# Latent attention of a diffusion layer on one core: values in three split passes, normalisation moved to the output, scores in four PSUM banks

## The reference

```python
def one_block(qi):                      # 128 queries, all heads
    s = jnp.einsum('bqkgd,bskd->bkgqs', qi, k).astype(jnp.float32) * scale
    p = jax.nn.softmax(s, axis=-1).astype(v.dtype)
    return jnp.einsum('bkgqs,bskd->bqkgd', p, v)
...
merged = jax.nn.sigmoid(ga) * (attn @ lp['w_branch_a']) + jax.nn.sigmoid(gb) * (pool @ lp['w_branch_b'])
x = x + gt1 * (merged @ lp['w_out'])
```

## Time and profile before

| | |
|---|---|
| median of 3 runs | 1750.43 us (1743.49 to 1750.63) |
| profiled execution | 1748.0 us, its span 1746.2 us |
| TensorE busy | 1593.9 us (91%) |
| VectorE, ScalarE, GpSimd busy | 899.4, 593.2, 287.0 us |
| latent attention | from about 614 to 1019 us of the span |

### The profile page before, as it was taken

The page is one execution under the profiler, slowest core; times in us unless marked ns, Lnnn a source line. Parts: engine busy times, 40 slices in busy tenths (PEclk is TensorE's granted clock), DMA queues, the critical chain, the costliest instruction groups (busy, mean ns, idle before and its releaser), DMA issues. The chain is left out here.

```text
span 1746.2 us, 21787 instructions
## 1 busy us (share of the span) xinstructions
PE 1593.9 (91%) x8173; PEld 1260.8 (72%) x8173; DVE 899.4 (52%) x1350; ACT 593.2 (34%) x776; POOL 287.0 (16%) x214
## 2 busy tenths in 40 slices
PE   4899999999998979999999999999997699999950
PEld 3688888788887756666666678887886588888840
DVE  6570000025654366667666653333455666676629
ACT  5212111233222354444444442111222255555513
POOL 1011111112324210001000000000000145444420
PEclk9999999999999989999999999999998699999985
DMA  9143333221001030003000024326003388998935
GB/s 363 70 154 130 143 149 141 91 90 44 24 24 61 1 115 1 0 0 145 1 0 0 1 86 148 138 73 230 36 37 133 128 276 269 285 300 262 283 72 230
DMA packets 48983, 206.60 MB, mean 118 GB/s; under 512 B 4913, under 2 KB 13985, under 8 KB 39713
## 3 DMA queue, kind: packets, MB, share of 16 engines
q1 hardware_dynamic: 39712, 172.30, 26.2%
q0 software_dynamic: 9216, 33.56, 8.6%
HBM read 158.60 MB, written 47.24 MB: 118 GB/s over the span
## 5 line engine op out<-in xcount | busy, mean ns | idle before, releaser
L343 PE MATMUL psum<-h_hi,w_hi 128*128 128x512 f32 (+1 forms) x768 | 201.6, 371 | 9.9 <-DVE h_lo L755 5.5
L343 PE MATMUL psum<-h_lo,w_hi 128*128 128x512 f32 (+1 forms) x768 | 193.4, 360 | 0.0
L343 PE MATMUL psum<-h_hi,w_lo 128*128 128x512 f32 (+1 forms) x768 | 192.8, 359 | 0.0
L1268 PE MATMUL psum<-probT,vals 128*128 128x512 f32 x384 | 190.9, 593 | 0.0
L1416 ACT ACTIVATE prob<-psum,nmax 128x1536 f32<-128x1536 f32 x64 | 98.7, 1542 | 199.7 <-DVE nmax L1544 199.5
L343 PEld LDWEIGHTS psum<-h_hi,w_hi 128*128 128x128 f32 x768 | 129.2, 191 | 39.0 <-issue 18.5
L1284 PEld LDWEIGHTS psum<-ident,prob 128*128 128x128 f32 x768 | 93.7, 142 | 77.7 <-issue 71.6
L343 PEld LDWEIGHTS psum<-h_lo,w_hi 128*128 128x128 f32 x768 | 128.8, 190 | 23.1
L343 PEld LDWEIGHTS psum<-h_hi,w_lo 128*128 128x128 f32 x768 | 128.4, 189 | 23.0
L1541 DVE TENSOR_REDUCE rmax<-psum 128x1 f32<-128x512 f32 x192 | 129.3, 689 | 24.6 <-PE psum L1260 24.4
L653 POOL TENSOR_TENSOR w_lo<-w_raw,w_hi 128x1024 fp32r<-128x1024 f32 x32 | 77.1, 2410 | 340.0 <-ACT w_hi L517 340.0
(11 more groups left out here) (330 smaller groups left out, 2885.7 us busy)
## 6 DMA issues: line engine op xcount, KB each, us to landing
gu_raw<-in_w_gu SPq DMA_DIRECT2D x16, 2048.0 KB, 9.2
ada<-in_w_ada SPq DMA_DIRECT2D x20, 1024.0 KB, 4.8
w_raw<-in_w_in SPq DMA_DIRECT2D x16, 1024.0 KB, 4.8
dn_raw<-in_w_dn SPq DMA_DIRECT2D x16, 1024.0 KB, 6.8
gates<-gst SPq DMA_DIRECT2D x14, 640.0 KB, 3.0
y_sum<-stage SPq DMA_DIRECT2D x12, 512.0 KB, 5.6
xt<-in_x SPq DMA_DIRECT2D x10, 512.0 KB, 8.0
merged<-gates SPq DMA_DIRECT2D x8, 640.0 KB, 3.9
```

Of the source, the lines that this page charges most:

```text
L343: mm = pe.matmul(psum[:, par_sets[j] + g:par_sets[j] + g + w], a[j][:, k, :], b[:, k, g:g + w], start=(k == 0 and a is w_hi and b is h_hi) ...
L1268: mm = pe.matmul(psum[:, PV + 512 * x.par:PV + 512 * x.par + 512], vals[:, x.key0 // P + c, x.kv * HD:(x.kv + 1) * HD], probT[b][g % 2][:] ...
```

## The change

What it does:

- Values: the value tile is split into `v_hi` and `v_lo`, the turned probabilities into `pT_hi` (a copy on ScalarE, all three banks) and `pT_lo` (a subtraction on VectorE). Each chunk's product is three float32r passes. The last pass raises `a_pv_unit` itself. All outputs go to one bank.
- Normalisation: the probabilities stay as the exponential leaves them. One reciprocal of all four sums of a unit on VectorE; TensorE transposes each, read as a 128x128 tile by broadcasting, into bank 3 (SPREAD), ScalarE copies that to `inv_row`, and VectorE multiplies the output with it into `qT`.
- Scores: banks 0 to 3. An even head uses 0, 1, 2; an odd one 3, 1, 2 in that order of keys, so the first third of a head is written while the exponential before still reads.
- The maximum of the first two banks is taken before the third; scale and last maximum are one instruction.
- Values of the first group are split before unit 0 is done, those of the second in the step of unit 8 (`second`).
- Buffers move: the late gates, the raw pool inputs. SP's queue loads fewer of them early, and pool inputs 2 and 3 after unit 14 is turned; three waits are added ahead of merge loads.

The diff, cut to its core:

```diff
-        SC, TP, PV = 0, 1536, 3072
+        TP, PV, SPREAD = 2048, 3584, 1536
...
         def scores_at(x, g):
-            return SC + 1536 * (isinstance(x.u, int) and x.u == 0 and g % 2)
+            return g % 2 * (2048 if first_unit(x) else 512)
+        def keys_at(g, b):
+            return 512 * ((b + 2) % 3 if g % 2 else b)
...
@@ SP
-                for q in range(4):
+                for q in range(2):
                     sp.dma_start(wb_raw[q][:], io["w_merge_b"][q]).then_inc(b_in[q], 16)
...
+                sp.dma_start(pool_raw[0][:], io["poolT"][0]).then_inc(loaded[0], 16)
+                for b in range(3):
+                    sp.wait_ge(s[f"a_turned{b}"], GRP * 15)
+                for k in range(2, 4):
+                    sp.dma_start(pool_raw[k][:], io["poolT"][k]).then_inc(loaded[k], 16)
...
@@ TensorE
+                    if not first_unit(x):
+                        if g == 1:
+                            pe.wait_ge(s["a_row"], x.u)
+                        pe.wait_ge(s["a_exped"], 4 * x.u + g - 1)
...
                     for b in range(3):
+                        if b == 1 and not first_unit(x):
+                            pe.wait_ge(s["a_exped"], 4 * x.u + g)
...
-                    pe.wait_ge(s[f"a_t_out{b}"], m + 1)
-                    mm = pe.matmul(psum[:, PV + 512 * x.par:PV + 512 * x.par + 512], vals[...], probT[b][g % 2][:], ...)
-                    mm.then_inc(s[f"a_pv{b}"], 1)
-                    if c == x.keys // P - 1:
-                        pe.wait_ge(s[f"a_pv{b}"], m + 1)
-                        pe.sem_inc(s["a_pv_unit"], 1)
+                    if c == 0:
+                        pe.wait_ge(s["a_v_lo"], GRP * (x.kv + 1))
+                        pe.wait_ge(s["a_pv_out"], x.u + 1)
+                    pe.wait_ge(s[f"a_t_hi{b}"], m + 1)
+                    pe.matmul(o, v_hi[v], pT_hi[b][g % 2][:], start=(c == 0), stop=False)
+                    pe.matmul(o, v_lo[v], pT_hi[b][g % 2][:], start=False, stop=False)
+                    pe.wait_ge(s[f"a_t_lo{b}"], m + 1)
+                    mm = pe.matmul(o, v_hi[v], pT_lo[b][g % 2][:], start=False, stop=last)
+                    if last:
+                        mm.then_inc(s["a_pv_unit"], 1)
...
-                            pe.wait_ge(s[f"a_t_out{b}"], uses(x, g))
+                        pe.wait_ge(s[f"a_t_lo{b}"], uses(x, g))
...
                 def tail(x):
+                    pe.wait_ge(s["a_inv"], x.u + 1)
...
+                    for h in range(GRP):
+                        o = SPREAD + h * P
+                        mm = pe.transpose(psum[:, o:o + P], einv[:, x.par, h:h + 1].broadcast_to([P, P]), ident[:])
+                    mm.then_inc(s["a_spread"], 1)
                     for c in range(x.keys // P)[-3:]:
                         values(x, c)
...
@@ ScalarE
+                def step(w, x, n, second=False):
+                    for g in range(GRP):
+                        high(w, 3 * g + 1)
+                        high(w, 3 * g + 2)
+                        if g < GRP - 1:
+                            high(w, 3 * g + 3)
+                            head(x, g + 1)
+                        if second:
+                            v_high(1, g)
+                    row(w)
+                    if n is not None:
+                        head(n, 0)
+                    high(x, 0)
...
@@ VectorE
+                def step(w, x, n, second=False):
+                    for g in range(GRP):
+                        low(w, 3 * g + 1)
+                        if g < GRP - 1:
+                            head(x, g + 1)
+                        elif n is not None:
+                            head(n, 0)
+                        low(w, 3 * g + 2)
+                        if g < GRP - 1:
+                            low(w, 3 * g + 3)
+                        if second:
+                            v_low(1, g)
+                    inverse_sums(x)
+                    out(w)
+                    low(x, 0)
```

More of the change, by code:

```diff
@@ L106, in build @@
         eps = small("eps", [P, 1])
+        neg_scale = small("neg_scale", [P, 1])
         ssq = small("ssq", [P, TILES])
@@ L706, in _ @@
                 own.step(nc.vector.memset(eps[:], EPS))
+                own.step(nc.vector.memset(neg_scale[:], -SCALE))
                 dve.sem_inc(s["eps_r"], 1)
@@ L997, in chunks, with over_units @@
             return range(3 * g, 3 * g + 3)
[L999 to L1017, removed]
+        def over_units(eng, prologue, step, epilogue, own=None, per=0, merge_weights=lambda: None):
+            prologue()
             for kv in range(KV):
@@ new lines, in prologue, with pool_high @@
+                def prologue():
+                    act.sem_inc(s["a_row"], 1)
+                    for g in range(GRP):
+                        head(units[0], g)
+                        v_high(0, g)
+                    head(units[1], 0)
+                    high(units[0], 0)
+                def pool_high(k):
+                    act.wait_ge(s["a_scored"], 12 * 16)
+                    act.wait_ge(loaded[k], POOL_IN)
+                    nc.scalar.copy(pool_hi[:, k, :], pool_raw[k][:]).then_inc(s["m_pl_hi"], 1)
@@ L1432, in merge_weights, with epilogue @@
+                def epilogue(x):
+                    for g in range(GRP):
+                        high(x, 3 * g + 1)
+                        high(x, 3 * g + 2)
+                        if g < GRP - 1:
+                            high(x, 3 * g + 3)
+                        pool_high(g)
+                    row(x)
                 def merge_weights():
@@ L1514, in split, with step @@
                     nc.gpsimd.tensor_tensor(q_lo[x.par][:], q, q_hi[x.par][:], ALU.subtract).then_inc(s["a_q_lo_r"], 1)
-                def head(x, g):
-                    if g == 0 and (not isinstance(x.u, int) or x.u):
-                        split(x)
+                def step(w, x, n, second=False):
+                    if n is not None:
+                        split(n)
                 def merge_weights():
@@ L1523, in _ @@
                 pool.wait_ge(s["a_q_lo_r"], 1)
-                over_units(pool, head, lambda x, g: None, lambda x, g: None, lambda x: None, merge_weights=merge_weights)
+                over_units(pool, lambda: split(units[1]), step, lambda x: None, merge_weights=merge_weights)
                 for j in range(2):
@@ L1537, in head @@
                 def head(x, g):
[L1539 to L1544, removed]
@@ L1546, in block_ @@
[L1546 to L1555 removed]
+                    at_ = lambda b: psum[:, scores_at(x, g) + keys_at(g, b):scores_at(x, g) + keys_at(g, b) + 512]
@@ L1557, in merge_weights, with epilogue @@
+                def epilogue(x):
+                    for g in range(GRP):
+                        low(x, 3 * g + 1)
+                        low(x, 3 * g + 2)
+                        if g < GRP - 1:
+                            low(x, 3 * g + 3)
+                    pool_low(0)
+                    out(x)
                 def merge_weights():
```

182 lines of the change are left out of this document (120 added, 62 removed).

## The result

The changed kernel takes 1729.2 us (median of 4 runs, 1727.19 to 1730.58) against 1750.53 (median of 4, 1743.49 to 1750.92): a ratio of 0.9887, 95% interval 0.986 to 0.9913. The profiled execution took 1728.98 us, its span 1727.1, so 19.1 us less than the span before.

A forecast was written before the change was run, and what follows sets the result against it. TensorE's own instruction stream was taken to bound the attention stage. The terms 18.6 + 11.1 + 2 - 6.9 - 1 - 0.5 - 0.5 - 0.3 gave 22.5 us, so 1748.0 - 22.5 = 1725.5 us, range 1708 to 1742.

The forecast's parts named there:

- stream of three passes: Value products on TensorE as three float32r passes, the first behind transposes 0.32 us, others 0.23: 18.6 us gained.
- collision with GpSimd: VectorE's value-split subtractions, both inputs in SBUF, held up by GpSimd's query split: 0 to 4 us lost, 0.5 taken.
- Rival 1: No restart penalty: the value pass behind transposes runs at 0.23 us, gaining 33.0 us; time 1711, chance 0.12.
- Own wait: TensorE's wait for its own last product at a unit's end goes: 11.1 us gained, 1 kept by loop edges.
- Spread: Four more TensorE transposes in each unit, for the inverse sums: 6.9 us lost.
- Ring and late low part: ScalarE and VectorE's ordered queues: ring 5.18 us under TensorE's 5.71 a head, low part's slack 0.4; cost nothing.
- Start: Start of attention, bound by VectorE and ScalarE: normalisations leave, low parts come in; 2 us gained, bounds 0 and 3.8.
- Four banks: Fourth score bank and rotated odd heads: nothing gained in the steady stage, only slack for the ring.
- End and queues: VectorE's last product delays pool parts before the merge: 0 to 0.7 us lost, 0.3 taken; SP's queue costs nothing.
- rival 2: The ring binds: slower handovers make ring and low part cost 0.2 to 0.3 us a head; 1738, chance 0.13.
- Rival 3: The passes gain nothing: 0.74 us a unit stays at its end, half the pass gain is lost; 1746, chance 0.08.
- rival 4: Slower: the ring becomes the attention stage's bound, at 6.4 us a head; 1769 us, chance 0.05.

The follow-up runs named there:

- e3: The kernel before, with only TensorE's wait for its own last value product removed: that product raises the unit's semaphore itself; 1741.84 us, ratio 0.9947.
- e1: The changed kernel, with GpSimd's query split also waiting for the last exponential of the unit two before; 1716.21 us, ratio 0.9819.
- e2: The changed kernel, with last maximum and scale (L1624) as one tensor-scalar instruction, the scale a constant instead of a tile; 1715.56 us, ratio 0.9809.
- e6: On e1, only one of a unit's four spread transposes made, so three heads are multiplied with leftover bank contents; 1720.41 us, ratio 0.9838.
- e4: The changed kernel without rotation and fourth score bank: all heads in banks 0 to 2; 1729.55 us, ratio 0.9883.
- e9: The changed kernel with the one-tile maximum of e2 and without rotation or fourth score bank, as in e4; 1718.14 us, ratio 0.9812.
- e7: The changed kernel with both the later query split of e1 and the one-tile maximum of e2; 1715.77 us, ratio 0.9813.

## Why the forecast came out right

The time was inside the range and 3.7 us from the forecast, but that is luck: two mechanisms were wrong and their errors cancel. The stream of three passes gained 12.8 us more than was taken, and waits for low parts that were put at next to nothing cost 12 us, 9.6 of them by the collision with GpSimd. Outside the stage 5.7 us were lost, where 0.3 had been taken.

- *Stream of three passes* (18.6 taken, bounds 15.7 and 33.0). Wrong, it was the upper bound. 0.862 + 0.435 became 1.135 a chunk, and the two chunks without transposes 0.69: 10 x 0.162 + 2 x 0.172 = 1.96 us a unit, 31.4 in all. The step that failed is the choice of 0.32 for the first pass while 0.43 was kept for the transposes ahead of it. The 0.43 had been measured in front of a float32 product, the 0.32 behind transposes in front of a float32r pass. The kernel before had the other half of that transition beside the rows that I read (timeline of TensorE):

```profile
709.78 1.50 PE L1284 MATMUL psum<-ident,prob 128*128 128x128 f32 x12 [0.40 <-PE psum L1268]
```

  Twelve transposes from 709.78 to the pass at 711.03 are 1.25 us, where 3 x 0.435 is 1.31 and 12 x 0.111 is 1.33. Both sides of the transition together carry no penalty. Rival 1 named the stream rightly, with a chance of 0.12.
- *Own wait* (11.1 less 1 for the edges). e3 gives 10.2, and there the edges keep nothing. In the changed kernel they keep something: at each of the four edges inside the loops the next unit's transposes start 0.44 to 0.49 behind the last pass (here 728.59 to 729.07), 0.21 to 0.26 more than a pass takes, and at the other units' ends hardly more than a pass. That is 0.9 us in all, what the prediction had set aside. e1 and e2 have it in the same places. The profile names no releaser there; what it is stays open.

```profile
728.59 0.39 PE L1281 MATMUL psum<-pT_lo,v_hi 128*128 128x512 f32 x1
729.07 1.17 PE L1295 MATMUL psum<-ident,prob 128*128 128x128 f32 x9
```

- *Spread* (6.9 lost). 16 x 0.445 = 7.1 of TensorE's time is right as a piece of the stream; e6 shows that without the collision leaving three quarters of it out gains nothing.
- *Ring and late low part* (nothing, slack 0.5 and 0.4). The ring is 5.32 and a head 5.46 (735.93 to 741.39), slack 0.14, because both sides were off: the ring by 0.14 up, the head by 0.25 down. It held, but any small delay now reaches TensorE: of the 1.05 us that L1624 lost, 0.91 arrived there (746.63, where 745.72 was due).
- *Collision with GpSimd* (0.5, for `v_low` only). Wrong, 9.6 by e1 and 10.1 by e2. I had the mechanism, gave it a price of up to 2.2 us, and looked for it only at the large subtractions of the values. Those were never held (mean below, whole span, for about 0.5 forecast each). The instruction that was held is the smallest of the added ones; its two streams are a column of `rmax` and the scale, which the change had put into a tile of one column, and it stands in each head. I had counted it as 0.22.

```profile
L1648 DVE TENSOR_TENSOR v_lo<-vals,v_hi 128x384 fp32r<-128x384 f32 x8 | 4.4, 554 | 4.3 <-ACT v_hi L1473 4.3
```

- *Start* (2 gained). 634.19 - 614.72 against 635.05 - 617.35, the first transposes of the stage: 1.8 gained. The same collision is there too (L1624 took 1.23 at 630.08).
- *Four banks* (nothing in the steady stage). e4 and e9: nothing.
- *End and queues* (0.3 lost, the rest nothing). The merge lost 1.7. VectorE's late pool part is 0.5 of it, as bounded; the other 1.1 is TensorE waiting for `merged` (1.4 us, where before only 0.3 stood). Part of that may have the same cause; no run takes it out. VectorE's product with the row waits for the last value pass, so its other pool parts start 1.0 behind the stage's end (998.02) where they had started 0.2 ahead of it (1019.02), and the gates for `merged`, which SP loads only behind VectorE's low parts, start 1.2 later too: 6.9 us behind the stage's end, where it was 5.75. The forecast didn't have that path. The same wait is 0.6 in e1 and 1.9 in e7, whose merge is the same code, so its size is partly chance. Group of TensorE, 985 to 1080 us:

```profile
L1339 PE MATMUL psum<-pool_hi,wb_hi 128*128 128x512 f32 (+1 forms) x96 | 24.1, 360 | 1.9 <-DVE merged L1725 1.4 <-DVE pool_lo L1678 0.5
```

The sum with what was measured, for the stage: 31.4 + 10.2 - 0.9 - 7.1 + 1.8 - 2.5 (the three waits for low parts that stay in e1) - 9.6 = 23.3, where 24.8 was measured; 1.5 us stay open. The sign that the prediction had set for rival 2, TensorE waiting for a low part, did appear, but its cause was another than rival 2's (the ring came out 0.14 us above its sum, still inside a head; a maximum was held up by GpSimd). Had I read the sign alone, I would have taken rival 2 as confirmed. e1 and e2 tell the two apart. Rival 3 fell with e3 (the wait's 0.68 a unit do go) and with the stream; rival 4's ring came to 5.32 us and not 6.4.

The best kernel of the runs that leaves nothing out is e2, 1715.56 us, ratio 0.9809 (0.9796 to 0.9823): one instruction of the changed kernel in another form. e1 and e7 are as fast.

## What to carry to other kernels

Measure a transition in a stream from both sides: what the first instruction behind it loses, and what the last ones ahead of it gain. A known contention must be looked up for every added instruction by its operands, not by its size; one over 128x1 elements, held because a constant had been put into a tile, cost 10 us because it stands on the path from scores to exponential and shares its releaser with GpSimd's work. And when a stream gets shorter, compare the new period with every ring that it ran ahead of: here the slack went from forecast 0.5 to 0.14 us, so that a further 44 us taken from TensorE were worth 3.

## What the runs showed of the hardware

- VectorE's instruction with two SBUF streams of one column, started behind GpSimd's subtraction of 128x512: 1.27 us instead of 0.22, and 0.22 where it started 0.05 us ahead of it. The same function with one stream, the scale a constant: 0.21, at the same place.
- Transposes (float32, 128x128) are 0.111 us apart in a stream: twelve ahead of a pass take 1.25 us (729.07 to 730.32) and four 0.36 (720.85 to 721.21). In front of a float32r pass a group is 0.09 us shorter, and that pass 0.09 longer: no net cost of changing between them. Four in front of a float32 product are 0.43.
- VectorE's subtraction of 128x512 with one operand in PSUM takes 0.685 us (192 of them), 0.60 behind another, as forecast from the earlier trace rows; two of them ran beside GpSimd's subtraction in e2 (743.92 to 745.20, the subtraction from 743.76 to 745.06) and took 1.28 together, as elsewhere.
